# Forgetting attention beside panel projections: five PSUM banks dealt four and one, the reciprocal moved up, and the steps paired

## The reference

```python
def odd_mixer(h, w_in, b_f, w_out):
    q, k, v, f = split_cols(h @ w_in, ODD_SPLITS)            # 1024, 1024, 1024, 16
    log_f = jax.nn.log_sigmoid((f + b_f).astype(jnp.float32))
    o = forgetting_attention(q, k, v, log_f)                  # 16 heads of 64
    return o.reshape(bsz, seq, FOX_W) @ w_out

def forgetting_attention(q, k, v, log_f):
    cum = jnp.transpose(jnp.cumsum(log_f, axis=1), (0, 2, 1))
    # for each block of 128 queries:
    s = jnp.einsum('bqhd,bshd->bhqs', qb, k) * scale
    s = s + (cq[..., :, None] - cum[..., None, :])
    p = masked_softmax(s, kpos[None, :] <= tpos[:, None])
    return jnp.einsum('bhqs,bshd->bqhd', p, v)
```

## Time and profile before

| | us |
|---|---|
| median of 3 runs | 2474.75 (2473.82 to 2474.89) |
| the profiled execution, its time | 2472.68 |
| its span in the trace | 2470.9 |
| mean granted PE clock | 0.986 of 2.4 GHz |
| PE busy | 2375.5 (96%) |
| DVE busy | 1435.2 (58%) |
| ACT busy | 1043.4 (42%) |
| POOL busy | 347.8 (14%) |

### The profile page before, as it was taken

How to read it: one execution, slowest core, us unless ns; L and a number is a source line. 1 busy time by engine, 2 the same in 40 slices (tenths; PEclk the granted TensorE clock), 3 DMA queues, 4 the chain that set the end, 5 groups by cost and what they waited for, 6 DMA issues and landing times.

```text
span 2470.9 us, 31530 instructions
## 1 busy us (share of the span) xinstructions
PE 2375.5 (96%) x11850; PEld 1913.6 (77%) x11862; DVE 1435.2 (58%) x2350; ACT 1043.4 (42%) x1788; POOL 347.8 (14%) x324
## 2 busy tenths in 40 slices
PE   8999899999999999799999999989999999999998
PEld 7877788888887777688888867767888767678887
DVE  3545655655655666556556458847533568666333
ACT  3656654322334555443233334444422344445223
POOL 0000111000000333210000127301100133101001
PEclk9999999999999999899999999999999999999999
DMA  5211003343332111133433322110322222102321
GB/s 190 100 52 44 2 28 105 141 153 120 132 124 94 52 52 52 36 119 133 149 120 146 112 71 74 60 35 27 103 94 95 85 69 69 43 27 69 111 94 51
DMA packets 58036, 211.73 MB, mean 86 GB/s; under 512 B 6432, under 2 KB 6560, under 8 KB 57888
## 3 DMA queue, kind: packets, MB, share of 16 engines
q1 hardware_dynamic: 57456, 208.86, 24.3%
q10 hardware_dynamic: 432, 0.85, 0.1%
HBM read 207.60 MB, written 2.10 MB: 85 GB/s over the span
## 4 chain that ended last, share of the span: by engine, by line
PE 79%; DVE 9%; issue 6%; ACT 4%; POOL 1%; DMA 0%; ACTq 0%; SPq 0%; DVEq 0%; POOLq 0%
PE bank L462 72%; PE last_bank L462 5%; PE bank L472 2%; DVE arena L1163 1%; DVE arena L2432 1%; DVE small L2102 1%; ACT arena_r L2080 1%; DVE arena L2434 1%; DVE arena_r L2107 1%; DVE arena L1019 1%; ACT wparts L573 1%; DVE small L838 0%; DVE wparts L577 0%; POOL rstd L632 0%; DVE arena_r L591 0%
## 5 line engine op out<-in xcount | busy, mean ns | idle before, releaser
L462 PE MATMUL bank<-hT,wparts 128*128 128x512 f32 x5520 | 1330.5, 397 | 6.1 <-DMA cb_sb<-cb_dram 4.4
L462 PEld LDWEIGHTS bank<-hT,wparts 128*128 128x128 f32 x5520 | 1034.8, 190 | 239.0 <-issue 23.6
L577 DVE TENSOR_TENSOR wparts<-ring,wparts 128x1024 fp32r<-128x1024 f32 x290 | 368.9, 1272 | 407.3 <-ACT wparts L573 406.7
L462 PE MATMUL bank<-arena_r,wparts 128*128 128x512 f32 x2400 | 553.6, 391 | 0.0
L462 PEld LDWEIGHTS bank<-arena_r,wparts 128*128 128x128 f32 x2400 | 451.1, 189 | 94.2 <-DVE arena_r L607 0.8
L573 ACT ACTIVATE wparts<-ring 128x1024 fp32r<-128x1024 f32 x332 | 348.2, 1050 | 158.2 <-PE bank L462 125.5
L577 POOL TENSOR_TENSOR wparts<-ring,wparts 128x1024 fp32r<-128x1024 f32 x42 | 101.3, 2413 | 214.0 <-ACT wparts L573 213.9
L603 ACT ACTIVATE arena_r<-arena 128x512 fp32r<-128x512 f32 x76 | 47.7, 630 | 178.7 <-POOL arena L2991 91.7
L462 PE MATMUL last_bank<-arena 128*128 128x64 f32 x780 | 106.4, 272 | 8.0 <-DVE arena L861 4.4
L472 PE MATMUL bank<-cf_sb,arena 128*128 128x128 f32 (+4 forms) x624 | 100.2, 281 | 14.3 <-DVE arena L1019 6.0
L462 PEld LDWEIGHTS last_bank<-arena 128*128 128x128 f32 x780 | 98.6, 193 | 16.6 <-issue 11.5
(11 more groups left out here) (294 smaller groups left out, 2397.7 us busy)
## 6 DMA issues: line engine op xcount, KB each, us to landing
ring<-weights_dram SPq DMA_DIRECT2D x388, 512.0 KB, 3.4
arena<-x_dram SPq DMA_DIRECT2D x4, 512.0 KB, 5.8
out_dram<-arena SPq DMA_DIRECT2D x4, 512.0 KB, 4.0
rot<-rot_dram SPq DMA_DIRECT2D x1, 512.0 KB, 10.8
rot<-rot_dram ACTq DMA_DIRECT2D x1, 512.0 KB, 3.2
cf_sb<-cf_dram SPq DMA_DIRECT2D x1, 416.0 KB, 9.1
cb_sb<-cb_dram SPq DMA_DIRECT2D x1, 264.0 KB, 10.1
vecs<-vec_dram ACTq DMA_DIRECT2D x1, 258.5 KB, 5.8
```

Source lines behind the costliest of these rows:

```text
L462: i = pe.matmul(*args, **kw)
L577: eng.tensor_tensor(wparts[:, slot, 1, :, :], ring[:, p % RAW, :, :], wparts[:, slot, 0, :, :].bitcast(F32), ALU.subtract)\
```

## The change

Three edits, all in the stage above.

1. The pools of attention: s and t get four banks (3, 4, 5, 6), and outputs one (7).
2. On DVE the reciprocal of map i-1 stands right behind its maximum, ahead of the low part of map i-3.
3. The list `order` for the six pairs of heads: 17 steps as before, 9 of panels and 8 of attention, but attention steps always stand two together, and panel steps two or three together.

```diff
         M1 = len(maps)
-        S1, O1 = POOLS[1:]
+        S1, O1 = (3, 4, 5, 6), (NBANK,)
...
                     dve.tensor_reduce(mx1(j), banks["fox", "s", j][:, 0:W], AX.X, ALU.max, negate=True)\
                        .then_inc(*dve_made.mark(("fox", "max", j)))
+                    dve.wait_ge(*act_made["fox", "p", j])
+                    dve.reciprocal(sm1(j), sm1(j)).then_inc(*dve_made.mark(("fox", "inv", j)))
                 if 3 <= i < M1 + 3:
                     j = i - 3
                     dve.wait_ge(*act_made["fox", "hi", j])
                     dve.tensor_tensor(fox_turned(j, 1), turned_map(j), fox_turned(j, 0).bitcast(F32), ALU.subtract)\
                        .then_inc(*dve_made.mark(("fox", "lo", j)))
                     banks.drain(("fox", "t", j), "dve_made")
-                if 1 <= i < M1 + 1:
-                    j = i - 1
-                    dve.wait_ge(*act_made["fox", "p", j])
-                    dve.reciprocal(sm1(j), sm1(j)).then_inc(*dve_made.mark(("fox", "inv", j)))
...
-        order = [0, 0, 0] + spread(6, 8) + spread(9, 8) * (KD - 2) + [0]
+        order = [0, 0, 0] + spread(6, 8) + [0, 0, 1, 1, 0, 0, 1, 1, 0, 0, 1, 1, 0, 0, 0, 1, 1] * (KD - 2) + [0]
```

## The result

The changed kernel takes **2497.13 us** (median of 4 runs, 2493.57 to 2499.0), the kernel before 2474.28 beside it (4 runs, 2473.76 to 2474.89). The ratio is 1.0093, with a 95% interval from 1.008 to 1.0106. The change costs 22.85 us. The prediction had 12.5 more, and its range ended at 2493: the direction was right, the size was not. The profiled execution of the changed kernel is the shortest of its four, 2493.57, with a span of 2491.8, 20.9 longer than that of before.

What follows compares the result with a forecast made beforehand. The prediction took DVE's chain, with ACT's answers inside, as the bound. Rounds of 32.3 us for 29.5 made the stretch 13.9 longer; less reciprocal gains, +12.5 was added to the median 2474.75: 2487.3 us, range 2477 to 2493.

Steps and rivals of the forecast that it cites:

- The rival by which the gaps close: PE bounds the round and loses its 2.0 us of idle time per round: 2463 us, chance 0.04.
- that by which DVE's chain stays whole: PE runs ahead, DVE's waits at drains stay hidden, only the reciprocals gain: -6 us, 2469, chance 0.10.
- the half: DVE and PE are coupled, but one of two detours is covered: +1 to +5 us, 2476 to 2480, chance 0.12.
- 1: End of group D: drain of v, then from a 256-wide map's maximum to the start of o: 2.87 us.
- Point 2: PE's o, s, 9 matmuls of q and turned values, ACT's high part, DVE's low part, hand-overs: 6.09 us.
- 3: DVE's long and short attention steps, out, drain of q and split: 6.15 us.
- 4: Way to the round's second o: 2.27 us.
- 5: PE's o, s and 15 matmuls of k with hand-over, DVE waiting some 2.4 for k's drain: 5.79 us.
- point 6: DVE's drain, two attention steps, out, split and four L591: 9.17 us, PE's 24 matmuls of v ending about 1 before.
- The clock falls: New PE gaps lower its granted clock, costing +12 to +25 beside the +12.5: about 2500 to 2512 us, chance 0.06.

Runs made afterwards that it cites:

- shifted pairs: Changed kernel with one panel step more ahead, so an output's low part is made in the pair before its own: 2467.12 us.
- shifted pairs with three banks: The paired order moved by one attention step, but with the kernel before's three banks for maps and two for outputs: 2473.42 us.
- the later drains: Changed kernel with the drains of k and v one attention step later, on DVE alone: 2477.63 us.

## Why the prediction was off, point by point

**What bounds the kernel: right.** The stage was bound by DVE's chain with ACT's answers in it. Four banks, which help PE alone, changed nothing (2474.84), and the reciprocal, which shortens the chain, gained. The rival by which the gaps close, and that by which DVE's chain stays whole, fell with the result; so did the half.

**The chain of waits: right in each point but one.** The prediction's six distances, from the drain at 879.39 to the one at 913.40:

| point | predicted | measured | from |
|---|---|---|---|
| 1 | 2.87 | 2.89 | 879.39 to 882.28 |
| 2 | 6.09 | 7.66 | 882.28 to 889.94 |
| 3 | 6.15 | 6.14 | 889.94 to 896.08 |
| 4 | 2.27 | 2.27 | 896.08 to 898.35 |
| 5 | 5.79 | 5.78 | 898.35 to 904.13 |
| 6 | 9.17 | 9.27 | 904.13 to 913.40 |
| round | 32.3 | 34.01 | |

Point 2 holds output, scores, 9 matmuls of q and the turn, all matmul work at the clock of before. The first of the six rounds begins with the output of head 0, which kept the clock: it is 29.68 (drains of v at 815.73 and 845.41), 29.5 predicted. In the other five, point 2 is 1.57 too little, which is 7.9 us. The sixth fall is at the end of the stage: the wait ahead of the last turned values was 1.74, predicted 0.15, since the output and the turn (1.05 where it took 0.60) ran at the low clock there too. Together 9.4, of the 23.9 - 13.5 = 10.4 by which the end of the stretch was missed; the last 1.0 is 0.1 at a time in other points. The loss of the clock is a term that my sum didn't have.

**The step that failed** is the one that put the clock's cost at nothing: the rival "The clock falls" got a chance of 0.06, and no term of the sum holds it. It rested on this sentence: "In the new round a stretch of 4 us around a gap has over 2 us of work, more than the one that kept 2.4 GHz." That came from "PE waits about 1.8 us ahead of each o". The wait is 1.54 in group B, but 2.62 in D. The longer gap could be had from the prediction's own numbers. Its point 6 says that in D DVE comes last, PE having ended the 24 matmuls about 1 us before. The gap ahead of o in D is therefore 2.87 - 1.2 + 1.0 = 2.7 and not 1.8. I worked out the gap of one group and wrote "each".

With the right gap the sentence falls. The 4 us that end with the output of D hold 1.39 us of work (878.28:882.28 above) and not over 2. The row that had kept the clock holds about as little, when it is cut so that it too ends with an output, in the kernel before:

```profile
812.12:816.12 4.00, 1.42 (x6) 0.70 (x5) 2.79 (x7) 1.72 (x5) 0.00 (x0) 1.00 0.00 0
```

So that row would have spoken neither for the fall nor against it. For it spoke the row at 998 (clock 0.65 behind 3.5 us), and one of the same trace that I did not read. Behind gaps of 2.09 (ahead of a t at 1025.07) and 1.41 an output took 2.61 us, at a clock of 0.50:

```profile
1027.13 2.61 PE L462 MATMUL last_bank<-arena_r 128*128 128x512 f32 x8 [1.41 <-DVE arena_r L2107]
```

A comparison of busy time around a gap could not have settled it either way, as the last section shows. But nothing on record was a ground for a chance as low as 0.06.

The price that the rival named was of the right size: up to 2.08 at a place, and 1.57 was measured. It was taken twice a round, where the fall comes once. 6 x 1.57 beside 12.5 would have given 2496.7.

**Smaller points.** PE's wait ahead of the s of a step 13 was 1.37, predicted 1.4. DVE's wait for the drain of k was 2.48, predicted 2.4. Its wait ahead of the turned values was 3.56: 2 as predicted, and 1.57 of clock on top. The wait of PE of 3.5 ahead of the last turn is gone, as predicted. The reciprocal was undervalued: 0.56 a round and 5.1 in all (4.5 and 0.6 on the last map) were predicted, 0.98 and 7.2 were measured. L591 and L577 became shorter, which no term held; POOL's overlap with them is the likely reason. In the changed kernel L591 has a mean of 686 ns too, so the gain is in its time and is covered by the loss.

**What stays open.** Why the clock falls behind one gap and not behind another like it (last section); why shifted pairs have 29.4 and not 28; and what shortened L591 and L577 when the reciprocal moved, since doubling POOL's work gives back only 0.16 of 0.73 us a round.

## What to carry to other kernels

When steps of two in-order streams are grouped, look for a result and its consumer that fall into the same group on different engines: their wait has lost the work that covered it, and shifting the grouping by one step can give it all back (2497.1 to 2467.1 here). Work out each new idle gap of the matrix engine place by place, with who comes last there, before the clock is judged, and do not count on the clock because one gap of that length kept it. And a cheap reordering within one engine may matter more for what runs beside what than for its place on the chain: list the neighbour engine's operation that it releases and see what that will overlap.

## What the runs showed of the hardware that was not expected

**The clock.** Neither the length of a gap nor the work just ahead of it tells whether the clock falls. The kernel with the order alone shows it within one execution. Windows over the 3.3 us that end at a t in group C, behind its wait of 1.72, and over the 1.7 us behind its start, in one round and in the next:

```profile
875.00:878.29 3.29, 1.56 (x12) 1.24 (x10) 1.29 (x2) 0.92 (x3) 0.00 (x0) 1.00 0.00 0
...
909.34:912.63 3.29, 1.57 (x11) 1.24 (x10) 1.29 (x2) 0.92 (x3) 0.00 (x0) 1.00 0.00 0
912.63:914.34 1.71, 1.49 (x10) 1.18 (x11) 0.69 (x3) 1.55 (x6) 0.95 (x1) 1.00 0.00 0
```

Behind 878.29 the clock is 0.66, behind 912.63 it is 1.00, with the same gap, the same work and the same busy time of every engine ahead. The kernel of shifted pairs with three banks does the same behind 1.34, and the changed kernel in two executions behind 3.00 and 2.95. In the order of this change the fall behind 2.62 came in all twelve rounds of two traces; behind 2.38, with the later drains, it came in none of six. When the fall comes must depend on more than these rows hold. What it costs is plain: 1.57 us in a round, 9.4 in the stretch by the trace, 11.4 by the difference of two medians. Ten matmuls of constants ahead of the wait kept the clock each time.

**DVE and POOL.** A DVE split of 1.23 us took 1.46 when a POOL multiplication had started 0.09 ahead of it (858.76), and 1.32 with 0.17 (859.33), but 1.23 with 0.50 (878.11 in the kernel before). POOL's 384 columns took 1.78 for 1.25 where they began inside a split.
